# Moving half of an mLSTM recurrence out of tile 0's routing and into its expert pairs, in a fused layer on one core

## The chip, the cores and the metric

The kernel runs on 1 core of a Trainium2 chip. The metric is device time in microseconds; the kernel before has a median of 3687.01 us over 3 runs (3683.57 to 3687.49).

## The reference, cut to what matters

One transformer-like layer for 128 context tokens and 1024 latent tokens, D = 1024: nine tiles of 128 tokens, tile 0 is the context.

```python
h  = modulate(rmsnorm(x))                        # per token
x += gate1 * W_out [ mLSTM(h) || attention(h) ]  # one input projection h @ W_in feeds both
x += gate2 * PEER(modulate(rmsnorm(x)))

# mLSTM: 4 heads of 128, forward over the tokens and backward over the tokens (a state C, n, m is
#        carried from chunk to chunk; the context's final state is an output, the latents start
#        from a cached one); h = h_f + h_b, normed per head, times a sigmoid
# attention: 8 query heads on 2 kv heads of 64. Context: softmax over its own 128 tokens and a
#        sink. Latents: 128 cached keys, +-128 neighbours and the sink
# PEER:  q = x @ w_q (8 heads x 256), scores against 2 x 128 sub-keys, top-16 of each, top-16 of
#        their 256 sums -> 16 expert ids and softmax gates per head: 128 experts per token
def blk(args):
    xb, eb, gb = args
    a = jax.nn.gelu(jnp.einsum('pd,phkd->phk', xb, u_tab[eb]))
    return jnp.einsum('phk,phkd->pd', gb * a, v_tab[eb])
```

Each token reads 128 rows of u and of v (4 KB each), 1.2 GB for all tokens.

## The kernel before, in words

Three blocks run one after the other. conditioning() and project_in() (to some 419 us) make the modulation and the input projections, and leave keys, values and queries of all tiles in SBUF or in DRAM scratch. mix_and_experts() (L654) does the rest, and only it is changed.

Its work is written as four kinds of step, and every engine has its own version of each, as a Python generator that emits that engine's instructions: mlstm() (a **cell** is one direction's step over one tile, 18 **units** u, three steps each and three at the end: 57 cell steps), mixer(t) (15 steps: attention, the norm of h, the product with w_out, x1), route(t) (51 steps: norm of x1, query product with w_q in chunks of 512 KB, sub-key scores, two halves of a top-16 choice) and pair(t, r) (64 a tile). drive() (L715) is called by each engine with its own four generators and so fixes one program order for all of them. The queues are in order: whatever an engine waits for, all that is behind it on that engine waits too. Engines meet through counting semaphores.

A **pair** is two expert slots of every token. GpSimd fetches the u and v rows (fetch(), L1109: two indirect DMAs of 1 MB into two of the eight ring buffers), VectorE does the two dot products with h2 (L1846), ScalarE takes gelu of them (L1538) and scales the picks (L1542), TensorE adds v's rows into acc (L1396), and that frees the two buffers: GpSimd waits for acc of pair n (s_acc) and then fetches pair n + 4 (DEPTH). The fetches of a tile's pairs 0 to 31 wait for the first half of the choice (s_route), those of 32 to 63 for the second.

The order before: six cell steps; the 15 steps of mixer(0) with a cell step at every odd k; 34 steps (PART) of route(0), with cells_beside(k) cell steps ahead of each (1 up to step 5, then two in three, then one or two); all cell steps that are left; begin(), where GpSimd waits for all h; then the pairs of nine tiles. Behind pair r of tile t come pace(t, r) steps of the routing (the second half of tile t's choice, then the first 34 steps of tile t+1) and, where due(t, r) holds, one mixer step of a later tile. In route(t), steps 6 to 13 and 20 to 27 are query chunks, 14 to 16 and 28 to 31 turn and score, 17 to 33 are the first half's choice (two top-16 of four lists, the sums, a top-16 of these, two "side" steps, ids and gates) and 34 to 50 the second half's.

SyncE issues the loads: load_cell(u) brings q and k transposed (512 KB), k and v (256 KB each, v in rows of 512 B) of a unit, load_h(t) the two directions' h that ScalarE's store_h(u) has put into DRAM, chunk(m) the w_q chunks of tiles 0 to 2 (two buffers, four for the first eight chunks). At pair 30 (WQ_AT) of tile 2, when all mixers are done, w_q as a whole (8 MB) is loaded into the room of the mixers' buffers, and tiles 3 to 8 read it there.

```python
def due(t, r):
    if t == STREAMED - 1:
        return r < WQ_AT
    return t == 0 and r < SUBS or 17 <= r < 23 or r >= 51 or r % 2

def pace(t, r):
    if t == STREAMED - 1:
        return int(r < 17 or r >= WQ_AT - 1) + int(r >= 48 and r % 2)
    return 1
```

## Time and profile before

| | |
|---|---|
| median of 3 runs | 3687.01 us |
| profiled execution, span from first to last instruction | 3682.8 us |
| TensorE matmul / VectorE / ScalarE / GpSimd busy | 2644.4 / 2453.7 / 990.0 / 1459.0 us |
| indirect DMA of the ring (q0) | 1208.03 MB, 78.4% of the DMA engines' time |
| all DMA | 1365.12 MB, mean 371 GB/s |
| mean granted TensorE clock | 0.865 of full speed |

The page has one execution. Its slices are of 92 us each; busy times overlap between engines, so that a wait counts only where it is the last to end. A row "x8" of matmuls is of two or four products, since each 32-bit product is issued as two instructions.

### The profile page before, as it was taken

The numbers are of one execution on the slowest core, as the hardware profiler recorded it, in microseconds if no ns is written. First come the engines' busy times: TensorE is split into PE (matmuls) and PEld (weight loads), VectorE is DVE, ScalarE is ACT, GpSimd is POOL, SyncE is SP. The second block draws the span as 40 slices with busy tenths as digits, with TensorE's granted clock in tenths as the row PEclk, the third lists the DMA queues.
The fourth block names the chain that finished last, engine by engine and source line by source line (L and its number), as shares of the span: only waits on it lengthen the run. The fifth ranks groups of instructions, "written<-read, shape, count | busy, mean of one in ns | idle before, by whom it ended". The sixth has DMA issues, their size and how long they took to land.

```text
span 3682.8 us, 31091 instructions
## 1 busy us (share of the span) xinstructions
PE 2644.4 (72%) x9770; PEld 1042.0 (28%) x9770; DVE 2453.7 (67%) x5523; ACT 990.0 (27%) x2700; POOL 1459.0 (40%) x1300
## 2 busy tenths in 40 slices
PE   7999888687877878866566567557656755775655
PEld 3455567333333333312121112112111211221111
DVE  3666435776787678648857677685767768576655
ACT  1223333442433244422122122212212221221111
POOL 0110023443454455434444444444444444444443
PEclk9999889899989989889799789879977987987677
DMA  7222446899999999999999999999999999999999
GB/s 299 95 97 94 163 125 204 333 410 422 416 421 426 425 412 420 389 424 414 427 427 427 427 423 427 422 417 424 416 427 420 427 420 423 424 417 427 411 427 380
DMA packets 224537, 1365.12 MB, mean 371 GB/s; under 512 B 25194, under 2 KB 36074, under 8 KB 75890
## 3 DMA queue, kind: packets, MB, share of 16 engines
q0 software_dynamic: 165888, 1208.03, 78.4%
q1 hardware_dynamic: 50992, 134.74, 10.1%
q10 hardware_dynamic: 7492, 20.36, 1.4%
q8 instruction: 77, 1.26, 0.1%
q14 instruction: 88, 0.72, 0.0%
HBM read 1334.05 MB, written 28.99 MB: 370 GB/s over the span
## 4 chain that ended last, share of the span: by engine, by line
DMA 40%; PE 20%; DVE 15%; issue 4%; POOL 4%; ACT 4%; SPq 0%; ACTq 0%; POOLq 0%; DVEq 0%
DMA fx_ring<-arg_uv,fx_eidx 38%; PE fx_acc L1396 11%; DVE fx_ring L1846 8%; POOL fx_ring L1109 4%; PE at_sP L1241 3%; ACT fx_weighted_pick L1542 2%; PE at_aP L1203 1%; DMA rt_wq<-arg_w_q 1%; DVE rt_rest L1708 1%; DVE rt_ab L1710 1%; DVE rt_rest L1706 1%; DMA rt_w_q<-arg_w_q 1%; PE at_sP L1269 1%; ACT fx_gelu L1538 1%; PE at_sP L1187 1%
## 5 line engine op out<-in xcount | busy, mean ns | idle before, releaser
L1396 PE MATMUL fx_acc<-fx_ring,fx_weighted_pick 128*64 128x512 f32 x4608 | 1417.7, 747 | 929.8 <-ACT fx_weighted_pick L1542 908.3
L1109 POOL DMA_INDIRECT fx_ring<-arg_uv,fx_eidx x1152 | 1317.0, 1143 | 1634.7 <-PE fx_acc L1396 1444.5
L1846 DVE CUSTOM_DVE_ANT_0 fx_ring<-fx_ring,fx_h 128x1024 f32<-128x1024 f32 x1152 | 1411.8, 1237 | 774.0 <-DMA fx_ring<-arg_uv,fx_eidx 769.5
L1396 PEld LDWEIGHTS fx_acc<-fx_ring,fx_weighted_pick 128*64 128x64 f32 x4608 | 327.0, 158 | 1903.7 <-ACT fx_weighted_pick L1542 1368.4
L1538 ACT ACTIVATE fx_gelu<-fx_dot 128x2 f32<-128x2 f32 x576 | 117.1, 203 | 2116.2 <-DVE fx_dot L1846 2115.7
L424 PE MATMUL in_z<-w_in,in_hT 128*128 128x512 f32 (+1 forms) x864 | 352.4, 566 | 7.3 <-PEq L97 7.3
L1542 ACT ACTIVATE fx_weighted_pick<-fx_weighted_pick,fx_gelu 128x64 f32<-128x64 f32 x1152 | 338.0, 340 | 55.1 <-ACT fx_gelu L1538 2.2
L424 PEld LDWEIGHTS in_z<-w_in,in_hT 128*128 128x128 f32 x864 | 163.6, 192 | 177.3 <-issue 172.0
L1269 PE MATMUL rt_qP<-rt_w_q,rt_h2T 128*128 128x512 f32 x384 | 193.6, 629 | 9.4 <-DMA rt_w_q<-arg_w_q 9.4
L384 POOL COPY in_turned<-in_heads 128x320 f32<-128x320 f32 x9 | 9.1, 1010 | 320.1 <-DVE in_heads L579 320.1
L1241 PE MATMUL at_sP<-at_w_out,at_mixT 128*128 128x512 f32 x288 | 133.3, 606 | 0.9 <-DVE at_mixT L1601 0.9
L1269 PEld LDWEIGHTS rt_qP<-rt_w_q,rt_h2T 128*128 128x128 f32 x384 | 66.8, 193 | 137.3 <-issue 126.3
L1838 DVE TENSOR_TENSOR fx_weighted_pick<-fx_pick,fx_gates 128x512 f32<-128x512 f32 x144 | 99.2, 689 | 2.4 <-DVE fx_gates L1729 0.7
L1846 DVE DVE_READ_ACCUMULATOR2_ANT fx_dot<- 128x1 f32 x1152 | 94.6, 82 | 0.0
L1560 DVE CUSTOM_DVE_ANT_0 at_s<-at_sP,at_mask,at_sink_negated 128x512 f32<-128x512 f32 x72 | 53.0, 750 | 60.7 <-PE at_sP L1187 50.9
L1538 ACT ACT_TABLE_LOAD x64 | 82.1, 1283 | 10.9 <-POOL ml_h L1129 9.7
L1269 PE MATMUL rt_qP<-rt_wq,rt_h2T 128*128 128x512 f32 x128 | 65.1, 632 | 15.1 <-DMA rt_wq<-arg_w_q 15.1
L1241 PEld LDWEIGHTS at_sP<-at_w_out,at_mixT 128*128 128x128 f32 x288 | 52.8, 191 | 78.1 <-issue 77.9
L1143 POOL TENSOR_TENSOR ml_k<-ml_k,ml_cols 128x512 f32<-128x512 f32 x18 | 18.7, 1039 | 141.2 <-ACT ml_cols L1506 108.9
L631 DVE SCALAR_TENSOR_TENSOR in_ada_acc<-in_ada_w,silu,in_ada_acc 128x1024 f32<-128x1024 f32 x56 | 70.1, 1292 | 0.3
L1203 PE MATMUL at_aP<-att_v,at_pT 128*128 128x64 f32 x432 | 67.8, 299 | 0.0
L1187 PE MATMUL at_sP<-att_kT,at_qT 64*128 64x384 f32 x144 | 65.4, 537 | 0.0
(300 smaller groups left out, 2450.4 us busy)
## 6 DMA issues: line engine op xcount, KB each, us to landing
rt_wq<-arg_w_q SPq DMA_DIRECT2D x44, 512.0 KB, 7.8
fx_ring<-arg_uv,fx_eidx POOLq DMA_INDIRECT x1152, 12.7
in_ada_w<-arg_w_ada SPq DMA_DIRECT2D x32, 512.0 KB, 4.0
ml_qkT<-qkT_scratch SPq DMA_DIRECT2D x18, 512.0 KB, 4.2
ada_w<-arg_w_ada SPq DMA_DIRECT2D x8, 1024.0 KB, 13.8
w_in<-arg_w_in SPq DMA_DIRECT2D x16, 512.0 KB, 16.4
rt_w_q<-arg_w_q SPq DMA_DIRECT2D x16, 512.0 KB, 32.7
kv_scratch<-in_kv ACTq DMA_DIRECT2D x9, 768.0 KB, 3.3
```

The source lines that it names most:

```text
L424: mm = pe.matmul(zp[b % 3][:, 0:n], hT[par][:, k, :], g.w_in[:, k, c0:c0 + n], start=(k == 0), stop=(k == KD - 1))
L631: dve.scalar_tensor_tensor(ada_acc[cnd][:], ada_w[m % AW][:], g.silu[:, k, cnd:cnd + 1], ada_b[:] if k == 0 else ada_acc[cnd][:], ALU.mult ...
L1109: pool.indirect_dma_start(out=ring[j][:], out_offset=None, in_=io.uv, in_offset=bass.IndirectOffsetOnAxis(ap=eidx[t % 2][:, i:i + 1], axis=0),
L1187: pe.matmul(ST[h % 2][:, P:4 * P], lhs, g.akT[half, t * P:t * P + 3 * P], start=True, stop=True).then_inc(s_sc, 1)
L1203: mm = pe.matmul(aP[:, h * ADH:(h + 1) * ADH], pT[h % 2][:, j * P:(j + 1) * P], rhs, start=(j == 0), stop=(j == 3))
L1241: mm = pe.matmul(ST[half][:], mixT[:, j, :], w_out[:, j, half * 512:(half + 1) * 512], start=(j == 0), stop=(j == KD - 1))
L1269: mm = pe.matmul(banks[half][b][:], hq2T[:, k, :], w[:, b * 512:(b + 1) * 512], start=(k == 0), stop=(k == KD - 1))
L1396: mm = pe.matmul(acc[b][cg * TOKS:(cg + 1) * TOKS, :], wsel[:, i % (2 * FILL), :], ring[i % GROUP][:, D + b * 512:D + (b + 1) * 512], star ...
L1538: act.activation(gelu[:, sl], dot[:, sl], ACT.Gelu_apprx_tanh).then_inc(s_gelu, 1)
L1542: last = act.activation(wsel[:, i, :], wsel[:, i, :], ACT.Copy, scale=gelu[:, i:i + 1])
L1838: dve.tensor_tensor(wsel[:, lo:lo + FILL, :], pick[:].unsqueeze(1).to_broadcast([P, FILL, TOKS]), gates[t % 2][:, r * NC:r * NC + FILL].un ...
L1846: dve.tensor_tensor_reduce(out=ring[j][:, 0:D], in0=ring[j][:, 0:D], in1=h2r[t % 2][cg][:], scale=1.0, scalar=0.0, op0=ALU.mult, op1=ALU.a ...
```

## The change

The mLSTM's cell steps are laid out anew: 16 in mixer(0), one ahead of each of the first six steps of route(0), none in steps 6 to 33, three behind begin(), one a pair in pairs 0 to 16 of tile 0 and two a pair up to pair 24. begin() no longer waits for the mLSTM. Mixer steps of tile 1 start at pair 25, route(1) at pair 40. So that cells and pairs can stand beside each other, the buffers in SBUF and the banks in PSUM are placed anew: the cells use the banks that only mixers use, tile 0's mixer and routing use acc's; tile 0's mixer has a set of buffers of its own (first), the later tiles another (later), and w_out and gate1 are loaded once for each. The scores of tile 0 are made over its own 128 keys alone, all heads at once, without the mask (context(k)). The first sixteen w_q chunks have up to six buffers. w_q as a whole is loaded at pair 41 of tile 2.

```diff
-    WQ_AT = 30
+    WQ_AT = 41
+    CELL_PAIRS = 25
     def due(t, r):
+        if t == 0:
+            return r >= CELL_PAIRS and (r < CELL_PAIRS + SUBS or r % 2 == 1)
         if t == STREAMED - 1:
             return r < WQ_AT
-        return t == 0 and r < SUBS or 17 <= r < 23 or r >= 51 or r % 2
+        return r % 5 != 4
     def pace(t, r):
+        if t == 0:
+            return int(r < 17) if r < CELL_PAIRS + SUBS else 1 + int(r % 3 == 0)
         if t == STREAMED - 1:
-            return int(r < 17 or r >= WQ_AT - 1) + int(r >= 48 and r % 2)
+            return int(r < 17) if r < WQ_AT - 1 else 1 + r % 2
         return 1
-    def ahead(m):
-        return 2 * WQ if m < HQ else WQ
-    def cells_beside(k):
-        if k < TURN:
-            return 1
-        if k < TURN + 11:
-            return int(k % 3 > 0)
-        return 1 + int(k % 4 > 0)
+    def buffer_of(m):
+        if m < HQ:
+            return m % 6
+        if m < NSIDE:
+            return (4, 5, 0, 1)[m % 4]
+        return m % WQ
+    def before(m):
+        return max((i for i in range(m) if buffer_of(i) == buffer_of(m)), default=None)
+    def cells_in_mixer(k):
+        if k < 4:
+            return 3 if k == 0 else 2
+        return int(k < 10 or k == SUBS - 1)
+    def cells_in_route(k):
+        return int(k < TURN)
+    def cells_in_pair(r):
+        return 1 if r < 17 else 2
     def drive(begin, pair, mixer, route, mlstm):
         cells = mlstm()
-        for _ in range(LEAD):
-            next(cells)
         subs = chain.from_iterable(mixer(t) for t in range(TILES))
         for k in range(SUBS):
-            if k % 2:
+            for _ in range(cells_in_mixer(k)):
                 next(cells)
             next(subs)
         steps = chain.from_iterable(route(t) for t in range(TILES))
         for k in range(PART):
-            for _ in range(cells_beside(k)):
+            for _ in range(cells_in_route(k)):
                 next(cells, None)
             next(steps)
-        for _ in cells:
-            pass
         begin()
+        for _ in range(3):
+            next(cells)
         for t in range(TILES):
...
                 for _ in range(min(pace(t, r), left)):
                     next(steps)
                     left -= 1
+                if t == 0 and r < CELL_PAIRS:
+                    for _ in range(cells_in_pair(r)):
+                        next(cells, None)
+                if t == 0 and r == CELL_PAIRS - 1:
+                    for _ in cells:
+                        pass
                 if due(t, r):
                     next(subs, None)
             for _ in range(left):
                 next(steps)
...
-        eP = acc[0][:].rearrange("p (h n) -> p h n", n=P)
-        oE = acc[0][:].rearrange("p (h n) -> p h n", n=256)
-        R = [x[:].rearrange("p (h n) -> p h n", n=256) for x in (acc[1], qP[0], qP[1])]
+        eP = other[0][:].rearrange("p (h n) -> p h n", n=P)
+        oE = other[0][:].rearrange("p (h n) -> p h n", n=256)
+        R = [x[:].rearrange("p (h n) -> p h n", n=256) for x in (other[1], qP[0], qP[1])]
         misc = cP[:].rearrange("p h n -> p (h n)")
-        qP0, cP0 = ST, aP[:].rearrange("p (h n) -> p h n", n=P)
+        first.ST, later.ST = acc, other
+        qP0, cP0 = acc, aP[:].rearrange("p (h n) -> p h n", n=P)
...
+                def load_weights(cnd):
+                    m = later if cnd else first
+                    sp.dma_start(m.gate1[:], g.gate_dram[cnd:cnd + 1, :].to_broadcast([P, D])).then_inc(s_g1, 16)
+                    for k in range(KD):
+                        sp.dma_start(m.w_out[:, k, :], io.w_out[k * P:(k + 1) * P, :]).then_inc(s_wo, 16)
                 def mixer(t):
+                    m = first if t == 0 else later
                     for k in range(SUBS):
                         if k == (3 if t == 0 else 0):
                             load_h(t)
+                        if k == 0 and t == 1:
+                            load_head(1)
+                            load_weights(1)
...
                 def begin():
-                    pool.wait_ge(s_hd, UNITS)
-                    for d in range(2):
-                        pool.wait_ge(s_hst[d], 16 * TILES)
+                    pool.wait_ge(s_x1o, 16)
                     for n in range(DEPTH):
                         fetch(n)
...
+                    def context(k):
+                        for b in range(2):
+                            for j in range(AH // 2):
+                                h = b * (AH // 2) + j
+                                half = slice(b * ADH, (b + 1) * ADH)
+                                cols_j = slice(j * P, (j + 1) * P)
+                                if k == 0:
+                                    mm = pe.matmul(m.ST[b][:, cols_j], m.aq[half, j, :], g.akT[half, P:2 * P],
+                                                   start=True, stop=True)
...
                 def begin():
-                    pe.wait_ge(s_hd, UNITS)
+                    pe.wait_ge(s_qT, NG)
+                    pe.wait_ge(s_h2d, NC)
```

## Rows read from the trace of the kernel before

**Rows 1.** The page's 40 slices of the span: DMA share in tenths, GB/s.
```profile
DMA  7222446899999999999999999999999999999999
GB/s 299 95 97 94 163 125 204 333 410 422 416 421 426 425 412 420 389 424 414 427 427 427 427 423 427 422 417 424 416 427 420 427 420 423 424 417 427 411 427 380
```

**Rows 2.** Stretches: length, busy us (count) by engine, clock, DMA share, GB/s.
```profile
424.00:664.00 240.00, 197.55 (x1116) 154.93 (x1116) 118.34 (x364) 79.55 (x245) 59.40 (x80) 0.85 0.53 178
578.00:664.00 86.00, 68.24 (x476) 54.94 (x470) 60.52 (x210) 27.69 (x98) 26.99 (x35) 0.96 0.53 175
664.00:682.00 18.00, 3.65 (x9) 0.91 (x9) 5.58 (x11) 0.79 (x3) 7.71 (x8) 0.50 1.01 388
682.00:764.00 82.00, 70.19 (x294) 32.30 (x294) 73.33 (x194) 38.78 (x85) 41.59 (x35) 0.92 1.01 413
664.00:3674.00 3010.00, 2049.84 (x7416) 689.84 (x7416) 2108.58 (x4764) 794.99 (x2262) 1363.08 (x1184) 0.85 1.01 420
```

**Rows 3.** The ring's fetches on GpSimd: all, and the ninth (of pair 4).
```profile
L1109 POOL DMA_INDIRECT fx_ring<-arg_uv,fx_eidx x1152: 932/940/2016, 664.1 to 3659.1; - x192
...
682.30 0.93 POOL L1109 DMA_INDIRECT fx_ring<-arg_uv,fx_eidx  x1 [8.37 <-PE fx_acc L1396]
```

**Rows 4.** The chain that ended last, in order of time: start, length, what.
```profile
470.24 2.02 DMA h_scratch<-ml_h
501.99 3.67 PE at_sP L1241 x8
537.60 3.50 PE at_sP L1269 x4
542.89 1.72 PE at_sP L1269 x4
```

**Rows 5.** VectorE's timeline, end of tile 0's mixer and its choice: start, length.
```profile
519.90 0.69 DVE L1610 TENSOR_TENSOR at_x<-at_x,at_xn 128x512 f32<-128x512 f32 x1
...
577.63 0.65 DVE L1617 MAX8 rt_val<-rt_scores 128x8 f32<-128x128 f32 x3
...
653.70 1.22 DVE L1706 TENSOR_TENSOR rt_rest<-rt_pos_partf,rt_iota 128x1024 f32<-128x1024 f32 x1
...
659.78 1.52 DVE L1718 SCALAR_TENSOR_TENSOR fx_eidx<-rt_ab 64x32 uint32<-64x32 f32 x4
...
661.80 0.79 DVE L1729 TENSOR_TENSOR fx_gates<-rt_gexp,rt_gsum 64x32 f32<-64x32 f32 x4
```

**Rows 6.** VectorE's groups of instructions, 577 to 663 us: busy, mean ns, idle before.
```profile
L1770 DVE SCALAR_TENSOR_TENSOR ml_c<-ml_c,ml_tile_decay,rt_qP 128x129 f32<-128x129 f32 x36 | 10.9, 344 | 4.7 <-PE rt_qP L1375 4.5
...
L1754 DVE TENSOR_TENSOR ml_e<-fx_acc,ml_e 128x512 f32<-128x512 f32 x9 | 6.2, 689 | 18.6 <-PE fx_acc L1366 14.6 <-issue 3.9
```

**Rows 7.** The same product of two cells with nothing between them, VectorE's timeline.
```profile
520.96 0.69 DVE L1754 TENSOR_TENSOR ml_e<-fx_acc,ml_e 128x512 f32<-128x512 f32 x1 [0.37 <-PE fx_acc L1366]
...
527.53 0.69 DVE L1754 TENSOR_TENSOR ml_e<-fx_acc,ml_e 128x512 f32<-128x512 f32 x1 [2.28 <-PE fx_acc L1366]
```

**Rows 8.** DMA of 424 to 664 us: packets, MB, share of the queue of SyncE's loads.
```profile
q1 hardware_dynamic: 21728, 37.77, 47.8%
```

**Rows 9.** Page: dot products; chain and timelines: acc twice, a table load, its activation.
```profile
L1846 DVE CUSTOM_DVE_ANT_0 fx_ring<-fx_ring,fx_h 128x1024 f32<-128x1024 f32 x1152 | 1411.8, 1237 | 774.0 <-DMA fx_ring<-arg_uv,fx_eidx 769.5
...
678.35 3.68 PE fx_acc L1396 x8
...
739.75 1.94 PE L1396 MATMUL fx_acc<-fx_ring,fx_weighted_pick 128*64 128x512 f32 x8
...
2143.99 1.28 ACT L1480 ACT_TABLE_LOAD   x1
2145.29 0.26 ACT L1480 ACTIVATE rt_gexp<-rt_gexp 128x64 f32<-128x64 f32 x1
```

**Rows 10.** w_q: landings of the streamed chunks in 690 to 1700 us; the wait for w_q.
```profile
DMA to landing us min/median/max: 7.5/8.1/14.6
...
  PE rt_qP L1269: 9.4, 1
```

429 lines of the change are left out of this document (244 added, 185 removed).

## The prediction

> **What bounds the kernel now.** I read the page first. Its slices show two stages: up to the eighth slice the share of the DMA engines is low and TensorE is the busiest engine; from there to the end the DMA line reads 9, at 410 to 427 GB/s but for one slice of 389 and the last [rows 1]. The chain that ended last says the same: 38% of it is one transfer, fx_ring from arg_uv. Then I cut the span into stretches [rows 2]: from 424 to 664 us the engines of the DMA are 0.53 busy, from 664 to 3674 us they are 1.01 busy at 420 GB/s. The first fetch is issued at 664.1 us [rows 3]. So the time is (first fetch) + (bytes after it, by the rate) + (stretches in which the DMA has nothing to do) + a tail of 9 us. 664.1 + 3018.7 = 3682.8 us, the span. The median of the runs is 3687.0, 4.2 more than the span (the runs lie 0.8 to 4.7 above it); I add 4.2 at the end.
>
> **Term 1, the first fetch comes earlier.** Before, tile 0's mixer ends at 520.6 us, its queries start at 537.6, the first top-16 starts at 577.6 and its first half is chosen at 662.6 [rows 4, 5]. After, no cell step stands between these from step 6 on.
> Steps 0 to 5 of the routing keep one cell step each, as before: 17 us, no change. Steps 6 to 13: eight chunks of w_q, 1.72 us each at the full clock and 3.50 for the first, which ran at half clock [rows 4]: 15.5 us. Steps 14 to 16 are one chain: copy 1.0, eight transposes 2.0, copy 0.6, scores 2.1, copy 0.6: 6.5 us. Steps 17 to 33 are VectorE's: in 578 to 664 it is 60.5 us busy [rows 2], of which the six lines of the cells take 33.6 (two of them in [rows 6], the others 7.5, 4.7, 2.5 and 1.8), which leaves 27; the steps one by one, from their first instruction to their last, give 32, since nearly every instruction waits for the one before; I take 32, and 3 for the two copies of h2 that wait for TensorE. Beside them TensorE has 24 us of rows, queries and scores. Sum 57 against 125 before (537.6 to 662.6): 68 us earlier.
> The mixer of tile 0: VectorE's gate scans up to 462 us and both directions' h, which must be stored (from 470 us on, [rows 4]) and read back, stay on the path: 3 us gained there, since the scores no longer stand before the store. Then four rounds of head pairs (score, turn, exp, values; TensorE alone takes 3.7 us for the values of one such pair) go, but two units of cells of 6.6 us [rows 7] now lie between k=4 and k=9, and three cell steps leave the w_out product. I get 8 to 13 us in all and take 11, less than the top because TensorE does less and so may run the first product at the lower clock.
> First fetch: 664.1 - 68 - 11 = 585 us: **-79** (bounds -64, if TensorE ran at half clock through the queries, and -89, if VectorE's 27 us were all).
>
> **Term 2, bytes that move behind the first fetch.** begin() no longer waits for the mLSTM. Of 57 cell steps 16 stand in the mixer, 6 in the routing, so loads of cells 9 to 17 (nine times 1.05 MB) and twelve stores of h (0.26 MB) come after the first fetch, where before all lay in the stage that is 0.53 busy. New is w_out's second load (4.2 MB), and gate1, aq and the mask of tile 1 move (1 MB). The hardware queue moved 37.77 MB in 47.8% of 240 us, 329 GB/s, in that stage [rows 8]: the 12.6 MB of the cells take 38 us; 5.2 MB in long rows, at 420, 12. **+50** (42 at 420 GB/s throughout, 58 if the 512-byte rows of ml_v cost more than that mean).
> The Trainium skill, DMA: Bandwidth & Descriptors (Where 436 GB/s comes from) puts the ports' limit at 435.2 GB/s; by it these 17.8 MB would be 41 us and the forecast 9 lower. The trace has 420 in the best long stretch, and the row decides.
>
> **Term 3, cell steps beside pairs of tile 0.** A pair: two dot products, 2.3 us of VectorE, then 0.9 us of ScalarE, then acc (1.94 us, 3.7 at half clock), then two fetches, 1.24 us apart [rows 9]. While one step a pair stands there (pairs 0 to 16) VectorE has 2.4 + 1.8 (routing, 30 us in 17 steps) + 1.2 (3.5 us a unit, 33.6 over nine and a half, [rows 6]): 5.4 us, and I find 5.6 with the one wait for GpSimd's select behind the fetches; the DMA needs 5.0 for the pair (2.1 MB at 420) and 1.4 for a third of a unit. The DMA stays the bound: +1 (0 to 20). With two a pair (17 to 24) I follow three pairs and two units in program order: the queues are in order, so finish(u) waits for the cell's products behind acc(r), which wait for Gelu behind Exp and a table load of 1.28 us [rows 9], and the select waits behind two fetches. Dot products of pairs 17 and 20 then start 27.4 us apart, 9.1 a pair; eight pairs 65 us, where the DMA has 54 us to do (40 for the pairs, 14 for three loads and five stores). **+11** (0 to 25).
> The Trainium skill, ScalarE: Activation LUTs (What ACT_TABLE_LOAD costs) gives 2.66 us for a switch, a drain of 1.38 behind the load. By it six switches here would cost 8 us more. In the trace the instruction behind the load starts 1.30 us after the load did [rows 9]: no drain is seen.
> Start of the pairs: cells 22 to 24 now stand before pair 0's dot products, GpSimd's part behind eight fetches; I get the fifth fetch 20.5 us after the first, against 18.2 [rows 3]; the eight transfers in flight cover it: 0.
> Pair 25 begins mixer 1, whose aq is loaded only after the last h is stored and h(1) is asked for (two landings of some 8 us, as in [rows 10]): TensorE stands some 13 us, but w_out's 4.2 MB are asked for then and keep the DMA busy: +2 (0 to 8).
>
> **Term 4, the routing of tile 1 ends too late.** Counting pace(): tile 0 has 17 steps in pairs 0 to 16, none up to 39, then 4 in three pairs: 32. 17 + 32 = 49 of 51, and two are left behind pair 63. Before, all were done at pair 50. The first half of tile 1 is chosen at the 34th of them, that is the last, and fetch 64, normally issued after acc(60), waits for it. When pair 63 has landed nothing is in flight: dot product 1.2, steps 30 and 31 (1.1, 3.75), steps 32 and 33 (3.7, 2.85; rows of tile 0's in [rows 5]), and 1.5 until the new transfers run: **+14.5** (10 to 20). In tile 2 the steps at pairs 40 to 63 are 1 and 2 by turns; the 34th falls in pair 62 (before: 57). Pair 61 holds both side steps (7.4 us beside 2.3), so pair 62's chosen half is ready 13.7 us after its data, pair 63's data 9.9 us after: **+5** (0 to 8).
> 4/3 query steps a pair from pair 42 on: a chunk lands in 8.1 us [rows 10] and two buffers give one in 4.3, the step comes every 4.5: +2 (0 to 10).
>
> **Term 5, w_q filled at pair 41.** Routing resumes at pair 40 and its first query is three pairs after the load begins (before: five). TensorE waited 9.4 us for it [rows 10], now perhaps 20, but four pairs of the ring and 8.4 MB of w_q are then in flight, 31 us and more: +1 (-3 to 5).
>
> The spreads of mixers over tiles 1 and 2 move no bytes and keep VectorE under 4.7 us a pair: 0.
>
> **Sum.** -79 + 50 + 1 + 11 + 2 + 14.5 + 5 + 2 + 1 = +7.5. Span 3690, time 3694 us. A measurement of this kernel tells about 0.2% (7.4 us) from no change, so the forecast sits on that bound.
>
> **Rivals.**
> A, *the lead of the ring covers the cells* (faster). If finish and select fall into VectorE's waits for landings (774 us of them in the whole, [rows 9]) pairs 17 to 24 cost only their bytes, and if the chain of the routing is nearer the 27 us of VectorE the first fetch is at 575 us. -11 -10, and the queries and pair 25 free, -4: 3694 - 25 = 3669. It decides when eight pairs with two cells take under 54 us. For it: landings cover much elsewhere. Against it: in 682 to 764 us VectorE is 73 of 82 us busy, 5.5 us a pair, with no cell steps.
> B, *the in-order chain is the bound in all 25 pairs* (slower). If acc and the cells' products run at half clock (0.50 in 664 to 682, [rows 2]) each unit adds some 5 us on TensorE to the chain, pairs 0 to 16 take 8 us rather than 6.4 and 17 to 24 11: +27 and +15, 3694 + 42 = 3736. Against it: with mixers beside pairs the clock was 0.92.
> C, *the start isn't gained*: without cells TensorE idles, the sixteen query steps run at 3.5 us and w_q's chunks of the second half come late: 20 us later, 3714. Against it: the cells' own products were a third of TensorE's time there.
>
> **Chances.** Forecast (3685 to 3703) 0.42, A 0.30, B 0.13, C 0.15. A is faster but for a tenth; the forecast's own spread lies half under +0.2%; B and C are slower. Faster 0.30, same 0.25, slower 0.45. Range 3662 to 3722, which leaves out most of B and the far end of A.
>
> **What would show it.** First fetch at 585 us (575 to 600); 17.8 MB more behind it and 3.9 MB more in all (w_out's second load less a mask); fetches of pairs 17 to 24 some 8 to 9 us apart; a gap of about 15 us in the DMA where pair 63 of tile 0 ends, and one of 5 where tile 2 ends, both with GpSimd's fetch released by fx_eidx's tile and not by fx_acc. It is wrong if the DMA stays at 1.01 through tile 0 (A), if pairs 0 to 16 take 8 us (B), or if the first fetch is after 600 us (C).

## The result: 1.2% slower, 3731.6 us against 3687.3

The changed kernel has a median of 3731.6 us over 4 runs (3726.9 to 3739.1), the kernel before 3687.3 us beside it. The ratio is 1.0124, with a 95% interval of 1.0109 to 1.0138: some 45 us slower. I had forecast 3694 us and a range up to 3722. The profiled execution has a span of 3731.5 us, which is the one read below; before's is 3682.8.

### The profile after

The page's slices answer to [rows 1]: before, the DMA line reads 9 from the ninth slice on; here it does so from the twelfth, with an 8 in the seventh, ninth and eleventh, and the GB/s dip to 370 to 379 three times after it.

```profile
DMA  7222548989899999999999999999999999999998
GB/s 295 98 98 86 189 140 335 357 349 411 343 414 406 416 377 408 370 395 412 379 427 426 426 421 427 419 425 422 414 427 418 427 416 425 423 421 427 413 427 367
```

The start answers to [rows 3, 4, 5]. These lines are tile 0's last addition of the mixer, the first product of its queries, and all fetches of the ring (min, median and max in ns, then first and last start).

```profile
501.51 1.29 DVE L1711 TENSOR_TENSOR at_x<-at_x,at_xn 128x512 f32<-128x512 f32 x1
...
521.06 2.90 PE L1341 MATMUL fx_acc<-rt_wq,rt_h2T 128*128 128x512 f32 x3 [1.69 <-ACT rt_h2T L1540]
...
L1160 POOL DMA_INDIRECT fx_ring<-arg_uv,fx_eidx x1152: 932/939/2033, 577.3 to 3707.9; - x192
```

The queries start at 521.1 us (before 537.6) and the first fetch is issued 56.2 us later, at 577.3 (before 126.5 later, at 664.1). So the start is 86.8 us earlier. Behind it stand 3154.2 us, where 3018.7 had stood.

Next are stretches cut at the first fetch of each tile, for the kernel before: tiles 0, 1, 2, then 3 to 8. The columns are those of [rows 2].

```profile
664.00:1022.00 358.00, 282.28 (x1176) 122.59 (x1176) 254.58 (x591) 137.82 (x325) 166.09 (x140) 0.91 1.01 415
1022.00:1377.00 355.00, 282.95 (x1179) 122.24 (x1178) 262.15 (x599) 139.56 (x334) 176.05 (x141) 0.91 1.01 422
1377.00:1737.00 360.00, 273.75 (x1064) 110.05 (x1062) 251.97 (x580) 117.24 (x296) 165.71 (x137) 0.90 0.99 412
1737.00:3674.00 1937.00, 1210.86 (x4002) 334.95 (x4000) 1339.88 (x2995) 400.37 (x1308) 855.23 (x768) 0.82 1.01 422
```

The same four stretches of the changed kernel:

```profile
577.00:1026.00 449.00, 316.36 (x1436) 154.96 (x1437) 289.74 (x683) 163.75 (x412) 188.72 (x180) 0.86 0.93 369
1026.00:1391.00 365.00, 300.91 (x1202) 130.38 (x1201) 258.79 (x597) 136.82 (x323) 167.73 (x140) 0.90 0.99 403
1391.00:1786.00 395.00, 309.36 (x1206) 132.96 (x1207) 266.28 (x610) 140.90 (x337) 164.12 (x140) 0.85 0.97 390
1786.00:3723.00 1937.00, 1238.52 (x4000) 338.75 (x3998) 1338.62 (x2992) 400.79 (x1308) 859.56 (x768) 0.80 1.00 421
```

(Pairs "fetched" in a stretch are released by the work of the pairs four earlier; stretches are named by the pairs fetched, steps by the pair they stand behind.)

All the loss in length stands in tiles 0, 1 and 2, which take 91, 10 and 35 us longer. Tiles 3 to 8 are alike.

To part bytes from stalls I take each stretch's bytes (length by GB/s) at 420 GB/s, the rate of the long stretch in [rows 2], and call the rest of its length its **stall**. All "stalls" below are worked out this way.

| stalls, us | tile 0 | tile 1 | tile 2 |
|---|---|---|---|
| before | 4 | -2 | 7 |
| after | 54 | 15 | 28 |

That is 88 us of new stalls, where my sum had 36.5. A stall in this sense isn't all idle DMA: by the DMA shares (1.01 where it is saturated) the DMA engines were idle for about 51 us more than before, and in the rest of the 88 they were busy but moved fewer bytes. The bytes came as forecast: 1281.97 MB behind the first fetch against 1264.40, or 17.6 MB for 17.8, which I count as 42 us, at 420. The queues of SyncE's and ScalarE's transfers in that stretch, which answer to [rows 8]:

```profile
q1 hardware_dynamic: 26254, 69.14, 5.6%
q10 hardware_dynamic: 1728, 3.15, 0.3%
```

Before, from 664 to 3674 us, there is no q10, and q1 is

```profile
q1 hardware_dynamic: 17424, 54.80, 4.6%
```

The account nearly closes: -87 + 42 + 88 = +43, of 48.7 in the spans. In tiles 3 to 8, equally long, 421 GB/s in place of 422 makes another 4.6, which is about what the rounding of these figures can make.

Where do the stalls stand? Here are five stretches of the changed kernel: the pairs with two cell steps (17 to 24, which release the fetches of 20 on), the wait for aq, the end of tile 0, pairs 48 to 55 fetched in tile 1, and pairs 16 to 23 fetched in tile 2.

```profile
703.00:778.00 75.00, 47.95 (x244) 27.77 (x242) 41.02 (x95) 26.95 (x72) 30.32 (x32) 0.83 0.77 286
782.00:798.00 16.00, 1.58 (x5) 0.86 (x4) 0.00 (x0) 0.18 (x1) 1.87 (x2) 0.50 0.97 393
1002.00:1026.00 24.00, 20.40 (x80) 8.67 (x79) 21.34 (x53) 8.83 (x19) 0.65 (x2) 1.00 0.60 232
1302.00:1353.00 51.00, 36.05 (x180) 18.12 (x180) 37.71 (x81) 28.21 (x57) 25.50 (x20) 0.93 0.93 363
1484.00:1537.00 53.00, 43.25 (x184) 22.82 (x184) 41.23 (x79) 28.46 (x60) 23.86 (x20) 0.77 0.91 356
```

In the first the DMA is 0.77 busy, although no engine is busy for more than 48 of 75 us: the engines wait for one another in turn. In the last two the work is that of pairs 44 to 51 and 12 to 19, where a mixer's attention steps meet the routing's choice steps, one of each behind a pair. There it is 0.93 and 0.91 busy.

The waits of the whole execution (total us, times, longest) that answer to [rows 10] and to the forecast:

```profile
POOL fx_ring L1160 <- DVE fx_gates L1830: 99.5, 3, 61.1
DVE at_s L1649 <- PE at_sP L1237: 72.5, 19, 19.4
DVE at_xn L1710 <- PE at_sP L1316: 68.4, 15, 9.5
DVE ml_e L1855 <- POOL ml_e L1200: 45.2, 8, 11.6
PE rt_qP L1341 <- DMA rt_w_q<-arg_w_q: 26.9, 1, 26.9
PE at_sP L1236 <- DMA at_qT<-aqT_scratch: 14.4, 1, 14.4
```

GpSimd's fetch waited three times for the gates: 61.1 us ahead of the first fetch, and 23.4 and 15.1 at the ends of tiles 0 and 2, as forecast. VectorE's waits for the mixers' scores and products are the ones that I had priced at nothing. Both rows lie wholly behind the first fetch. In the kernel before, the same two waits in its tiles 0 to 2 (664 to 1737 us) are

```profile
DVE at_s L1560 <- PE at_sP L1187: 41.5, 19, 7.1
DVE at_xn L1609 <- PE at_sP L1241: 41.0, 10, 7.7
```

so together they grew from 82.5 to 140.9 us (19.4 of that is the one wait at pair 25, behind aq).

### The profile page after: what moved, and what is told of

Its sections match the earlier page's. It is cut to its first block, busy times and chain, and to the rows that moved or that the text cites. A ratio compares the mean times of both kernels' runs of the same rounds, so it can differ in the third digit from the quotient of the medians.

```text
span 3731.5 us, 30884 instructions
## 1 busy us (share of the span) xinstructions
PE 2683.4 (72%) x9682; PEld 1041.3 (28%) x9682; DVE 2458.7 (66%) x5516; ACT 1003.4 (27%) x2707; POOL 1444.8 (39%) x1300
## 4 chain that ended last, share of the span: by engine, by line
DMA 38%; PE 21%; DVE 15%; POOL 5%; issue 5%; ACT 4%; SPq 0%; ACTq 0%; POOLq 0%; DVEq 0%
DMA fx_ring<-arg_uv,fx_eidx 34%; PE fx_acc L1471 12%; DVE fx_ring L1946 8%; POOL fx_ring L1160 5%; PE at_sP L1316 3%; ACT fx_weighted_pick L1630 2%; DMA rt_wq<-arg_w_q 2%; PE rt_qP L1341 1%; PE at_aP L1253 1%; DVE rt_rest L1809 1%; DVE rt_ab L1811 1%; DVE rt_rest L1807 1%; DMA rt_w_q<-arg_w_q 1%; ACT fx_gelu L1626 1%; PE at_sP L1237 1%
## 5 line engine op out<-in xcount | busy, mean ns | idle before, releaser
L1471 PE MATMUL fx_acc<-fx_ring,fx_weighted_pick 128*64 128x512 f32 x4608 | 1464.6, 769 | 874.9 <-ACT fx_weighted_pick L1630 846.1
L1160 POOL DMA_INDIRECT fx_ring<-arg_uv,fx_eidx x1152 | 1303.5, 1131 | 1804.1 <-PE fx_acc L1471 1513.5
L1341 PE MATMUL rt_qP<-rt_w_q,rt_h2T 128*128 128x512 f32 x384 | 193.6, 629 | 26.9 <-DMA rt_w_q<-arg_w_q 26.9
L1316 PE MATMUL at_sP<-at_w_out,at_mixT 128*128 128x512 f32 x256 | 123.3, 626 | 0.0
L1626 ACT ACT_TABLE_LOAD x71 | 91.1, 1283 | 1.3
L1503 ACT ACTIVATE at_s<-at_s,at_negmax 128x512 f32<-128x512 f32 x64 | 45.9, 718 | 54.4 <-DVE at_negmax L1649 54.0
L1253 PE MATMUL at_aP<-att_v,at_pT 128*128 128x64 f32 x384 | 57.5, 289 | 0.0
```

Source lines behind the costliest of these rows:

```text
L1160: pool.indirect_dma_start(out=ring[j][:], out_offset=None, in_=io.uv, in_offset=bass.IndirectOffsetOnAxis(ap=eidx[t % 2][:, i:i + 1], axis=0),
L1253: mm = pe.matmul(aP[:, h * ADH:(h + 1) * ADH], m.pT[h % 2][:, j * P:(j + 1) * P], rhs, start=(j == 0), stop=(j == 3))
L1316: mm = pe.matmul(m.ST[half][:], m.mixT[:, j, :], m.w_out[:, j, half * 512:(half + 1) * 512], start=(j == 0), stop=(j == KD - 1))
L1341: mm = pe.matmul(banks[half][b][:], hq2T[:, k, :], w[:, b * 512:(b + 1) * 512], start=(k == 0), stop=(k == KD - 1))
L1471: mm = pe.matmul(acc[b][cg * TOKS:(cg + 1) * TOKS, :], wsel[:, i % (2 * FILL), :], ring[i % GROUP][:, D + b * 512:D + (b + 1) * 512], star ...
L1626: act.activation(gelu[:, sl], dot[:, sl], ACT.Gelu_apprx_tanh).then_inc(s_gelu, 1)
```

## The experiments

"Changed" names the kernel after, "before" the kernel before. Each ratio is to runs of before on the same chip, with its 95% interval.

### What the cells cost beside the pairs

**All cells drained ahead of the pairs.**

```diff
+        for _ in cells:
+            pass
         begin()
-        for _ in range(3):
-            next(cells)
```

> The changed kernel, but all cell steps left after the routing of tile 0 (35 of 57) run before the first fetch, none beside pairs; everything from pair 25 on is as in the changed kernel. Draining them alone should take some 65 to 85 us, so the first fetch comes at about 650 us. By my prediction cells beside pairs cost the pairs 38 us of bytes and 14 us of stalls, 52 in all: first fetch to end 3102, time 3756. By the rival, that two cell steps or even one a pair hold the in-order chain for longer than the transfers last, they cost 70 us or more: first fetch to end 3084 or less, time 3738 or less. If the loss of tile 0 lies elsewhere (buffers, second load of w_out), pairs 0 to 24 stay above 5.8 us each even without cells.

Measured: 3750.2 us, 1.0162 (1.0147 to 1.0177). The fetches and tile 0:

```profile
L1160 POOL DMA_INDIRECT fx_ring<-arg_uv,fx_eidx x1152: 932/938/2028, 655.2 to 3718.3; - x192
...
655.00:1044.00 389.00, 267.48 (x1011) 103.56 (x1012) 250.68 (x572) 116.72 (x296) 153.15 (x137) 0.83 0.96 394
```

Drained alone, 35 steps put the first fetch off by 78 us, 2.2 us a step. First fetch to end is 3088 us, so beside the pairs these cells cost 3154 - 3088 = 66 us. That lies between the 52 of my theory and the rival's 70. Tile 0 still stalls by 24 us here without a single cell beside a pair, nearly all of it in pairs 56 to 63 (20 us).

**No pair with two cell steps.** 18 more steps are run before the first fetch; pairs 0 to 16 keep one each.

```diff
     def cells_in_pair(r):
-        return 1 if r < 17 else 2
+        return int(r < 17)
...
+        for _ in range(18):
+            next(cells)
         begin()
-        for _ in range(3):
-            next(cells)
```

> The changed kernel, but 18 more cell steps run before the first fetch (in place of 3 behind it and 15 as second steps in pairs 17 to 24), so that pairs 0 to 16 keep one cell step each and pairs 17 to 24 have none; mixer 1 and the routing of tile 1 stay at their pairs. Draining 35 steps took 78 us in the run with all drained, so 18 take some 38 to 42 and the first fetch comes at about 617. In the changed kernel pairs 17 to 24 took 80 us, 10.0 each, where I had worked out 65. If two cell steps a pair are the in-order chain's price, these pairs fall to about 42 us and pairs 0 to 16 stay at 97: first fetch to end 3154 - 38 = 3116, time 3731 to 3737. By the rival, that the loss there is of the whole stage of cells (clock, small packets), pairs 17 to 24 stay over 50 us and the time is over 3745.

Measured: 3730.8 us, 1.0114 (1.0095 to 1.0134). First fetch at 617.0, to the end 3112 us. The same eight pairs' work in this run, to be read against 703:778 of the changed kernel:

```profile
737.00:782.00 45.00, 23.52 (x64) 5.45 (x64) 20.33 (x34) 6.33 (x24) 19.03 (x17) 0.73 1.00 405
```

My expectation counted nine fetch intervals for eight pairs. From the fetch of pair 20 to that of pair 28 the changed kernel takes 75.3 us and this run 44.7, its DMA at 1.00. The sixteen fetches before them, of pairs 4 to 19, are the same in both, 101.7 and 102.3 us. So the two-cell pairs cost 31 us over none; 15 steps drained alone cost 33. Within the measurement, pairs with two cell steps gain nothing. The time is that of the changed kernel.

### The spread of the mixers, alone

The kernel before, with only the order of later steps, and the place of w_q's load, as in the change.

```diff
-    WQ_AT = 30
+    WQ_AT = 41
...
 def due(t, r):
...
-    return t == 0 and r < SUBS or 17 <= r < 23 or r >= 51 or r % 2
+    if t == 0:
+        return r < SUBS or r > SUBS and r % 4 == 1
+    return r % 5 != 4
 def pace(t, r):
...
-            return int(r < 17 or r >= WQ_AT - 1) + int(r >= 48 and r % 2)
+            return int(r < 17) if r < WQ_AT - 1 else 1 + r % 2
```

> The kernel before, with only the spread of the later steps changed as in the change: mixer steps 27, 52 and 41 over tiles 0, 1 and 2 (before 49, 41, 30), w_q filled at pair 41 of tile 2 instead of 30, tile 3's routing in pairs 40 to 63 at 1 and 2 steps by turns. Tile 0's routing of tile 1 and the first fetch stay. By my prediction this costs 5 (boundary of tiles 2 and 3), 2 (query steps) and 1 (w_q), nothing for the mixers: 3695. By the rival, a mixer step in four pairs of five beside a routing step makes those pairs longer than their transfers: tiles 1 and 2 together 30 to 40 us longer than before's 714, as in the changed kernel (761 with 3 MB more), time 3717 to 3727. If the loss in tiles 1 and 2 comes of the new buffers or queues of the changed kernel, this run stays below 3692.

Measured: 3717.7 us, 1.0086 (1.0071 to 1.0100): 28 us slower than before by the medians, 30 by the spans. The time is the rival's, not mine. Its tiles 0, 1 and 2:

```profile
663.00:1009.00 346.00, 249.00 (x984) 96.71 (x984) 240.73 (x558) 113.02 (x286) 150.40 (x136) 0.87 1.01 417
1009.00:1381.00 372.00, 302.89 (x1233) 130.29 (x1232) 265.32 (x609) 140.32 (x336) 168.45 (x141) 0.92 0.99 406
1381.00:1770.00 389.00, 301.34 (x1208) 128.05 (x1209) 265.98 (x610) 139.21 (x334) 165.89 (x141) 0.88 0.97 395
```

Stalls 3, 12 and 23 us, against 4, -2 and 7 of before. Tile 0, which gives up 22 mixer steps, is 12 us shorter, and tiles 1 and 2 are 46 longer. They stall here nearly as much as in the changed kernel (15 and 28), at the same places: 9 us in pairs 48 to 55 fetched in tile 1, 7 in 16 to 23 of tile 2, 9 in the last eight. No cell step stands beside a pair and no new buffer is in this kernel. So that part of the loss comes of the order of the mixer steps, the routing steps and w_q's load alone. This is the run that decides against my forecast's last line.

### Which engine holds a pair with a mixer step

**Half of the w_out product left out** in the mixers of tiles 1 to 8.

```diff
-    for j in range(4 * quarter, 4 * quarter + 4):
+    for j in range(4 * quarter, 4 * quarter + 4) if t == 0 else (4 * quarter, 4 * quarter + 3):
```

> The changed kernel, with two of the four matmuls left out in each w_out step of the mixers of tiles 1 to 8 (their output rows are then not the reference's): 1.85 us of TensorE less in four pairs of each mixer. If TensorE's place in the in-order chain (acc behind the w_out product) is what stretches pairs with a mixer step in tiles 1 and 2, the two are 8 to 15 us shorter, time 3718 to 3722. If VectorE's or GpSimd's part or the DMA decides there, the time stays within 4 us of 3731.

Measured: 3715.2 us, 1.0074 (1.0047 to 1.0102), its runs lying from 3703 to 3739. Tiles 1 and 2:

```profile
1035.00:1396.00 361.00, 273.44 (x1139) 118.58 (x1140) 257.63 (x597) 137.08 (x323) 170.46 (x141) 0.90 0.99 409
1396.00:1775.00 379.00, 285.39 (x1163) 120.75 (x1164) 266.00 (x610) 140.78 (x337) 163.59 (x140) 0.87 0.98 404
```

Stalls 10 and 14 us instead of 15 and 28. TensorE's part of the mixer stands in the chain. It was 0.82 busy at most in these tiles of the changed kernel (300.9 of 365 us), so I take it to be its place in the order and not its load; that is argued from the busy time. The gain isn't everywhere. In pairs 16 to 23 fetched in tile 2 the stall fell from 8 to 3 us; in pairs 48 to 55 of tile 1 it did not fall (8 for 7).

**The table loads taken out** of the attention, by Identity in place of Exp.

```diff
-    act.activation(m.s[h % 2][:], m.s[h % 2][:], ACT.Exp, ...
+    act.activation(m.s[h % 2][:], m.s[h % 2][:], ACT.Identity, ...
...
-    act.activation(m.es[:], m.es[:], ACT.Exp).then_inc(s_es, 1)
+    act.activation(m.es[:], m.es[:], ACT.Identity).then_inc(s_es, 1)
```

> The changed kernel with Identity in place of Exp in the attention of tiles 1 to 8 (their output rows are then not the reference's): ScalarE's time for it stays, but its switches of the table between Exp and Gelu go, some 40 loads of 1.28 us. If these loads stand in the in-order chain of pairs that hold an attention step (Gelu behind Exp), half of the 38 us by which tiles 1 and 2 stall more than before goes: 3711 to 3719. If TensorE's and VectorE's waits for each other are the chain and the loads fall beside them, the time stays within 5 us of 3731.

Measured: 3736.4 us, 1.0125 (1.0106 to 1.0143), the changed kernel's own ratio. The group of loads in front of Gelu on the changed page is x71, 91.1 us; here it is

```profile
L1626 ACT ACT_TABLE_LOAD  x41: 1283/1283/1283, 599.9 to 3482.5; - x41
```

These are thirty fewer, and the changed kernel's 31 loads in front of the attention's Exp (L1503) are gone too: 61 loads of 1.28 us less, and no gain. Half of the 38 us of stalls would have shown. That half the stall is theirs is refuted.

### Moving steps about in the changed kernel

**Mixer steps kept apart from choice steps**, at the same counts a tile.

```diff
 def due(t, r):
     if t == STREAMED - 1:
-        return r < WQ_AT
+        return 0 if 12 <= r < 18 or r >= WQ_AT else 1 + (r in (19, 21, 23, 25, 27, 29))
+    if t == 1:
+        return not (45 <= r < 51 or r in (4, 10, 16, 22, 28, 34))
     return r % 5 != 4
...
-                if due(t, r):
+                for _ in range(due(t, r)):
```

> The changed kernel with the same counts of mixer steps (27, 52, 41 over tiles 0, 1, 2) and the same routing, but mixer steps kept out of pairs 45 to 50 of tile 1 and 12 to 17 of tile 2, where VectorE has the choice of the best 16 (3.7 us a step); the other pairs take them up, six pairs of tile 2 from 19 to 29 with two. In the changed kernel the stalls in tiles 1 and 2 stand at pairs 48 to 55 (6.9 us) and 16 to 23 (8.0). If it is the meeting of an attention step and a choice step in one pair that costs, both go: 12 to 15 us less, 3718. If it is the number of mixer steps a pair that costs, wherever they stand, the stalls move to where the steps went: within 4 us of 3731, or slower.

Measured: 3752.4 us, 1.0166 (1.0147 to 1.0185), 21 us slower than the changed kernel. Pairs 16 to 23, then 24 to 31 fetched in tile 2:

```profile
1490.00:1537.00 47.00, 30.61 (x106) 10.26 (x106) 33.52 (x65) 21.43 (x47) 16.76 (x16) 0.72 1.01 425
1537.00:1599.00 62.00, 52.11 (x193) 24.72 (x193) 30.61 (x57) 19.02 (x44) 21.96 (x21) 0.85 0.72 263
```

The stall of 8 us in the first is gone; one of 23 us stands in the second, where four of the six doubled mixer steps fall. In tile 1 the stall of pairs 48 to 55 only fell from 7 to 6. There the fetches of pairs 45 and 46 came 12.6 and 10.2 us after the ones before them, released by acc of pairs 41 and 42, behind which an attention step and a choice step still stood; the transfers ran out in the fetches of pairs 47 to 49. A late fetch shows here as a stall two to three pairs later. So in tile 2 taking one of two meeting steps away removed the stall; putting it behind another pair brought one back, larger, also where the two are both mixer steps.

**Tile 1's routing earlier, two steps a pair.**

```diff
-            return int(r < 17) if r < CELL_PAIRS + SUBS else 1 + int(r % 3 == 0)
+            return int(r < 17) if r < CELL_PAIRS + SUBS else 2
```

> The changed kernel with two steps of tile 1's routing a pair from pair 40 of tile 0 on, in place of four in three pairs: the 34 steps end at pair 56, not behind pair 63. By my term for the boundary the gap of 10 us in the DMA where pair 63 ends goes, and the time is 8 to 12 us less, 3721. By the rival, steps crowded at two a pair make the chain of those pairs longer than the transfers, as much as was gained: pairs 40 to 56 take 6.5 us or more each and the time stays within 4 us.

Measured: 3746.9 us, 1.0157 (1.0144 to 1.0170), 15 slower. Pairs 48 to 55, then 56 to 63 fetched in tile 0:

```profile
907.00:986.00 79.00, 63.04 (x258) 28.87 (x259) 43.17 (x139) 24.64 (x55) 18.51 (x19) 0.83 0.81 310
986.00:1033.00 47.00, 36.67 (x159) 16.54 (x158) 32.67 (x65) 13.55 (x36) 20.91 (x19) 0.90 0.87 331
```

The stall of 16 us in pairs 56 to 63 became 20 us in pairs 48 to 55 and 10 in the last eight. The last step is no longer late, and it gained nothing. The streamed chunks of w_q don't explain it: TensorE waited 14.6 us for them from 880 us to the end of tile 0, and 15.6 in the changed kernel.

**Tile 3's routing, two steps a pair.**

```diff
-            return int(r < 17) if r < WQ_AT - 1 else 1 + r % 2
+            return int(r < 17) if r < WQ_AT + 1 else 2
```

> The changed kernel with the routing of tile 3 in pairs 43 to 59 of tile 2 at two steps a pair, in place of one and two by turns in 40 to 63. By my term for this boundary the gap of some 8 us in the DMA at the end of tile 2 goes, since the last step stands four pairs ahead; and with its first query three pairs later the routing waits less for w_q: 3722 to 3725. By the rival, which moving tile 1's routing ahead bore out (15 us slower), two steps a pair hold their pairs longer than the transfers and nothing or less than nothing is gained: 3731 to 3745.

Measured: 3756.7 us, 1.0178 (1.0160 to 1.0195), 25 slower than the changed kernel, more than the rival said. The profiled execution is the fastest of the five, 3744.4 us. In it pairs 40 to 63 fetched in tile 2 stall by 10, 8 and 11 us by eights, 29 in all, and by 14 in the changed kernel. But this run is no test of two steps a pair. With its first routing step at pair 43, the load of x1 for that step is issued behind the 16 loads of w_q of pair 41, and ScalarE stood for it, with the Gelu of the next pair behind:

```profile
1697.23 1.06 ACT L1529 ACTIVATE rt_scores<-rt_scores 128x1024 f32<-128x1024 f32 x1 [39.00 <-DMA rt_scores<-x_scratch]
```

In the changed kernel, whose routing resumes one pair ahead of w_q's load, no such wait stands there. The fetch of pair 47 came 41.9 us after that of pair 46, and the stalls of the fetches of pairs 47 to 49 are 10 us: two thirds of the 15 that this run has more.

### The two halves of the change, apart

**The old order in the new buffers.** The changed kernel's layout, short scores of tile 0 and second load of w_out, with before's order: all cells ahead of the first fetch beside the routing, mixers 49, 41, 30, w_q at pair 30.

```diff
-    WQ_AT = 41
+    WQ_AT = 30
...
 def cells_in_route(k):
-    return int(k < TURN)
+    if k < TURN:
+        return 1
+    return int(k % 3 > 0) if k < TURN + 11 else 1 + int(k % 4 > 0)
 # in drive: every cell step left is run before begin(); due() and pace() are before's
```

> The changed kernel's buffers, its short scores of tile 0 and its second load of w_out, with the order of before for everything else: all cell steps ahead of the first fetch beside the routing, mixer steps 49, 41 and 30 over tiles 0 to 2, w_q at pair 30, one routing step a pair. If the loss is all of the order, this run has the gain of the mixer (9 to 11 us) and the cost of 4.2 MB (10 us): 3684 to 3692. If the buffers or the second load cost more, 3697 or more.

Measured: 3671.9 us (3668.2 to 3678.5), ratio 0.9955 (0.9938 to 0.9972): **faster than before by 15 us**, outside what I expected on the good side, and faster than both kernels. All fetches, then tiles 0, 1 and 2:

```profile
L1158 POOL DMA_INDIRECT fx_ring<-arg_uv,fx_eidx x1152: 935/942/2079, 644.5 to 3643.2; - x192
...
644.00:1011.00 367.00, 285.56 (x1179) 123.12 (x1180) 257.51 (x596) 137.80 (x326) 171.85 (x141) 0.91 1.00 414
1011.00:1364.00 353.00, 279.05 (x1176) 119.02 (x1174) 261.08 (x599) 139.24 (x333) 172.80 (x140) 0.92 1.01 424
1364.00:1720.00 356.00, 274.64 (x1066) 108.85 (x1064) 251.16 (x579) 117.65 (x296) 164.64 (x137) 0.89 1.00 415
```

The first fetch is 19.6 us earlier than before's, tile 0 is 8 us longer (4.2 MB more are 10 us at 420), tiles 1 and 2 are 5 shorter. So the change's two halves have opposite signs: buffers and short scores give -15 us, the order takes 60 (3671.9 to 3731.6). Which of the layout's parts brings the first fetch forward by that much is not shown.

**Fewer cells beside pairs, the side steps spread more evenly.** 18 of the cell steps go back beside the routing of tile 0.

```diff
-    WQ_AT = 41
-    CELL_PAIRS = 25
+    WQ_AT = 36
+    CELL_PAIRS = 17
...
 def cells_in_route(k):
-    return int(k < TURN)
+    return int(k < TURN or k % 3 > 0)
 # pace(0, r): 0 in pairs 17 to 31, then 1, doubled at 32, 36, 40, 44, 48; pace(2, r): 4 in 3 from 35
# due(0, r): also at pair 62; cells_in_pair(r): 1
```

> The changed kernel with 18 cell steps put back beside steps 7 to 32 of tile 0's routing and 17 beside pairs 0 to 16; mixer 1 in pairs 17 to 31, tile 1's routing from 32 on at one step a pair and five doubled, done at pair 60; mixer steps 32, 52, 36 over tiles 0 to 2, w_q at pair 36, tile 3's routing at 4 in 3 pairs. By the account so far (two side steps a pair are what costs, and a last step behind pair 62): first fetch 577 + 18 x 1.6 = 606; behind it 15 us fewer of bytes, 22 fewer of stalls in pairs 17 to 31, 14 at the end of tile 0, 5 at the end of tile 2, 2 in tiles 1 and 2: 3154 - 58 = 3096. Time 3702. If the stalls only move, 3715 or more.

Measured: 3682.3 us (12 runs, 3679.0 to 3686.7), 0.9985 (0.9975 to 0.9994). First fetch at 609.8 (606 expected), to the end 3071.5 (3096 expected). The last eight pairs fetched in tiles 0 and 2:

```profile
962.00:1007.00 45.00, 39.17 (x132) 14.42 (x130) 35.82 (x82) 11.42 (x30) 19.00 (x16) 0.96 1.01 425
1697.00:1737.00 40.00, 30.95 (x108) 10.30 (x106) 39.23 (x90) 11.56 (x31) 17.17 (x16) 0.84 1.01 427
```

Both ends of tiles are clean, at four steps in three pairs in tile 2 and one a pair in tile 0. Tiles 1 and 2 stall by about 10 us in all, not 43, where I had given the move 2. Five mixer steps went from tile 2 to tile 0. Tile 1 keeps its 52 mixer steps and its one routing step a pair, at the same pairs; only which ones meet has moved by five. Behind pairs 45 to 50, where VectorE's longest choice steps stand, there are now the end of the attention and the w_out steps, and attention steps before. Tile 1's stall is -2 us for 15 (pairs 48 to 55: 2 for 7). It also starts from a clean end of tile 0. So the count of steps alone did not make that stall; which steps meet matters too. Tile 0 still stalls by 28: 8 in pairs 16 to 23 fetched, where cells meet choice steps, and 17 in 40 to 55, where doubled routing steps meet mixer steps. So it ends 10 us behind the run above.

**Five cell steps beside pairs, in the run with the old order.**

```diff
-        for _ in cells:
-            pass
         begin()
 def cells_in_pair(r):
-    return 1 if r < 17 else 2
+    return 1            # pairs 0 to 4; mixer 1 from pair 5, tile 1's routing from pair 20
# the rest is as in the run with the old order, but cells_in_route(k) leaves five cell steps over
```

> The run with the old order in the new buffers, but its last 5 cell steps stand beside pairs 0 to 4 instead of before the first fetch; mixer 1 follows in pairs 5 to 19, tile 1's routing in pairs 20 to 53, still 49 mixer steps in tile 0, none moved to tiles 1 and 2. By the sum: first fetch 8 us earlier (1.6 a step), bytes behind it 4 us more, 1 to 3 of stalls: within 4 us of that run, 3668 to 3675. If a cell step beside a pair costs no more than its bytes, 3668; if even one a pair holds the chain, and mixer steps moved into the pairs of tile 1's choice steps cost as well, 3680 or more: then the overlap pays nowhere.

Measured: 3683.3 us (12 runs), 0.9985 (0.9976 to 0.9995), 11 us slower than without. The first fetch came 4.5 us earlier, not 8. Tile 0 took 11 us longer, with 7 us of stall in pairs 16 to 23 fetched, and 7 more stand in 56 to 63 of tile 1; pairs 0 to 15, which hold the cells, stall by 3. The rival held: even five cell steps do not pay, and most of the price stands where the mixer steps were pushed to.

### Is it the number of steps, or which steps?

In the run with the old order, tile 3's routing is set to two steps a pair, with w_q long there and no mixer step left.

```diff
-    return int(r < 17 or r >= WQ_AT - 1) + int(r >= 48 and r % 2)
+    return int(r < 17) + 2 * int(r >= 43)
```

> The run with the old order in the new buffers, where tiles 1 and 2 stall by 2 us in all, with one edit: tile 3's routing stands at two steps a pair in pairs 43 to 59 of tile 2, instead of one a pair from 29 and a second now and then from 48. w_q is long there (filled from pair 30), no mixer step is left, and the last step is as early as before, so nothing but the number of steps a pair differs. If two routing steps a pair are by themselves longer than the transfers, as the run with tile 3's routing so doubled in the changed kernel suggests (28 us of stalls in pairs 40 to 63), the stalls of these pairs rise from 1 to 15 us or more: 3686 and up. If the stalls there were w_q's and the mixers', the time stays within 4 us of 3672.

Measured: 3691.1 us (12 runs, 3684.7 to 3699.8), 1.0012 (1.0002 to 1.0022), 19 slower than without the edit (15 in the spans). Of these 15 us only 8 are stalls of the edited pairs; the other half is spread over fetches ahead of them, which the edit does not touch, and I cannot say where it comes from. Pairs 40 to 47, 48 to 55 and 56 to 63 fetched in tile 2:

```profile
1592.00:1643.00 51.00, 25.50 (x64) 5.51 (x64) 21.06 (x34) 7.36 (x26) 17.02 (x17) 0.67 1.01 426
1643.00:1685.00 42.00, 37.53 (x164) 15.96 (x166) 23.54 (x51) 15.35 (x39) 19.33 (x16) 0.96 1.01 427
1685.00:1741.00 56.00, 41.07 (x158) 15.63 (x156) 53.17 (x150) 14.60 (x40) 15.90 (x17) 0.83 0.89 345
```

The first holds next to no side steps. The second, released behind pairs 44 to 51, holds the first half's eight query steps and does not stall at all: TensorE is 37.5 of 42 us busy, and the DMA is at 1.01. The third holds the choice steps (and the second half's query steps) and stalls by 10 us: VectorE is 53 of 56 us busy. Its timeline between the dot products of pairs 58 and 59 (1.2 us each, dot products L1944):

```profile
1720.54 1.22 DVE L1805 TENSOR_TENSOR rt_rest<-rt_pos_partf,rt_iota 128x1024 f32<-128x1024 f32 x1
1721.80 1.23 DVE L1807 TENSOR_TENSOR rt_rest<-rt_rest,rt_val 128x1024 f32<-128x1024 f32 x1
1723.06 1.22 DVE L1809 TENSOR_REDUCE rt_ab<-rt_rest 128x64 f32<-128x1024 f32 x1
1724.31 1.23 DVE L1944 CUSTOM_DVE_ANT_0 fx_ring<-fx_ring,fx_h 128x1024 f32<-128x1024 f32 x1
```

So the time is what the theory said, but the place is not, and these pairs' stalls rose by 8 us and not by 15. Two query steps a pair were free here and two choice steps weren't: from one pair's dot products to the next pair's they kept VectorE for 5.0 us behind pair 58 and 6.6 behind pair 59, beside 2.4 of dot products, and a pair's transfers take 5.0. Here, then, it is VectorE's time that runs out and not only its place in the chain. The last eight pairs of tile 2 in the changed kernel look alike (VectorE 52 of 53 us busy), so a part of the gaps at the ends of tiles is probably VectorE's; finishing earlier at two choice steps a pair would not remove it.

## Why the prediction was wrong, by its own steps

| term | forecast | measured |
|---|---|---|
| 1, first fetch | -79 | -87 |
| 2, bytes | +50 | +42 (at 420 GB/s) |
| 3, start of the pairs and pairs 0 to 16 | +1 | +5 |
| 3, pairs 17 to 24 and 25 | +13 | +27 |
| 4, end of tile 0 | +14.5 | +14 |
| 4, end of tile 2 | +5 | +6 |
| 4, query steps (pairs 32 to 55 of tile 0) | +2 | +3 |
| 5, w_q | +1 | +7 |
| spread of the mixers | 0 | +25 |

The measured stalls are those of eight pairs each, changed kernel less before; the last row is tile 1 (+17) and the first 40 pairs of tile 2 (+8). All rows sum to +43 before rounding; the spans differ by 48.7.

**Term 1** was right in its two parts. The routing took 56.2 us for the 57 worked out. The mixer gained 16.5 us for 11, above my bound of 13. Why it gained more is not shown; the layout alone, in the run with the old order, already brought the first fetch forward by 19.6.

**Term 2** was right in MB. Its price was not measured by itself: 42 is the MB at 420, and what small rows cost beyond that stands among the stalls. The time of the queues' own packets says more. By the rows above, q1 and q10 took (share times length of the stretch) 47 us more of the DMA engines than before, 43 to 52 by the rounding of the shares, for 17.5 MB, a rate of 371 GB/s, between the 329 that I had taken for the cells' part from [rows 8] and 420. So neither my 50 nor 42 is refuted. The Trainium skill's 435.2 GB/s (DMA: Bandwidth & Descriptors, Where 436 GB/s comes from) gave an estimate of 41 for my 17.8 MB. The trace does not bear out that rate itself: no slice of the page is above 427.

**Term 3**: the mechanism was right, the size was not. I had eight pairs with two cell steps take 65 us, 11 over their transfers; they took 75, and the stall of pairs 16 to 31 is 29.5 against 2. Most of that was a slip in my own sum: my 9.1 us a pair make 73 for eight pairs, not 65. I had followed three pairs with TensorE at full clock; the trace has a mean of 0.83 there. VectorE waited 8 times for GpSimd's select behind the fetches, 45.2 us in all, its dearest wait in the cells. The start, which I had at nothing, cost too: the fetch of pair 4 came 24.0 us after the first (20.5 forecast), with a stall of 5 us in the first eight pairs against 1 before. At pair 25 TensorE stood 14.4 us (13 forecast) while the DMA was 0.97 busy with w_out: right, and hidden as said.

**Term 4**: both gaps stood where I put them, with the fetch released by the gates. Finishing earlier gave the one at tile 0's end back only where the steps were not crowded to two a pair: crowded, the stall moved ahead and grew; with fewer doubled steps both ends were clean.

**Term 5**: TensorE waited 26.9 us for w_q where I had 20, and pairs 40 to 55 fetched stall by 6 us, before's by -1: +7 for +1.

**The step that failed** is the one sentence "The spreads of mixers over tiles 1 and 2 move no bytes and keep VectorE under 4.7 us a pair: 0." The row that answers to it is +25 here. In the run that changed the order of later steps alone the same pairs have +15, and with w_q's and the end of tile 2 the new stalls are some 28 us; so 15 of the 25 are shown to be the spread's own, and for the other 10 no run parts the spread from what tile 0 hands on. It argued from VectorE's busy time, and that was right as far as it goes: 259 of 365 us in tile 1. But a pair with a mixer step and a routing step is a chain through four engines in one order: acc of a pair stands behind the w_out product or the head pairs, VectorE's mask and x1 stand ahead of the next dot products and wait for them, and the two fetches wait for acc. I had followed this chain for pairs with cell steps, found it longer than the transfers, and did not follow it for pairs with mixer steps.

**Rival B** named nearly the time, 3736, and not the reason: pairs 0 to 16 cost 5 us and not 27, so the half clock in all 25 pairs isn't what happened, and its time is near by luck. The closest reading is probably my own forecast with the chain applied to all doubled pairs, which I have not worked out.

**The reading that holds** is: before, the 192 pairs of tiles 0 to 2 held 120 mixer steps and their routing so that they cost -2 to 7 us of stalls a tile. The change puts 35 cell steps into tile 0. They gain 2.2 us each against cells run alone, but only 0.9 to 1.9 against cells run beside the routing (78 us for 35 alone; 67 us from 644.5 to 577.3 for the same 35 beside it; 4.5 for the last five). Each costs 0.9 us in bytes (12.6 MB over 35), and it pushes 22 mixer steps into tiles 1 and 2 and the routing into the last third of tile 0, where attention steps meet long choice steps.

What stays open: how much of the stall of a pair with an attention step is TensorE's scores and how much its w_out product. Only the latter was thinned, with a wide interval, and it helped in tile 2's pairs 16 to 23 and not in tile 1's pairs 48 to 55. Nor was the w_q load at pair 41 ever moved by itself.

## What to carry to other kernels

When a DMA-bound loop has work of other stages woven in, its slack is not only engine time but the slack of the in-order chain in each iteration. Follow one iteration for every combination of side steps that the new order makes, also for those that only move. Work beside a saturated stage is no longer free once there is no iteration with room for it. Look also at what a moved step's own load now stands behind: one load of x1 behind w_q held ScalarE for 39 us. And when a change has two halves, time them apart: here the layout alone was worth 15 us, and the order took 60.
